# Two one-hot groups in a row ahead of every second expert tile, and four second-half scatter transfers between heads

## The reference, cut to what matters

```
idx = jnp.take_along_axis(cand_idx, top_pos, axis=-1)
gate = jax.nn.softmax(top_s, axis=-1)
u = expert_down[idx]
v = expert_up[idx]
act = jax.nn.gelu(jnp.einsum("td,thkd->thk", xb, u).astype(jnp.float32), approximate=False)
return jnp.einsum("thk,thkd->td", (gate * act).astype(v.dtype), v)
```

## Time and profile before

| | us |
|---|---|
| median of 3 runs | 1308.4 (1308.36 to 1309.39) |
| time of the profiled execution | 1307.0 |
| its span, first to last instruction | 1305.2 |
| PE busy | 1286.4 (99%) |
| PE weight loads busy | 1168.2 (90%) |
| DVE busy | 963.2 (74%) |
| ACT busy | 760.5 (58%) |
| POOL busy | 483.8 (37%) |

### The profile page before, as it was taken

The page is one execution under the profiler, slowest core; times in us unless marked ns, Lnnn a source line. Parts: engine busy times, 40 slices in busy tenths (PEclk is TensorE's granted clock), DMA queues, the critical chain, the costliest instruction groups (busy, mean ns, idle before and its releaser), DMA issues. The chain is left out here.

```text
span 1305.2 us, 25973 instructions
## 1 busy us (share of the span) xinstructions
PE 1286.4 (99%) x8501; PEld 1168.2 (90%) x8501; DVE 963.2 (74%) x1898; ACT 760.5 (58%) x1153; POOL 483.8 (37%) x276
## 2 busy tenths in 40 slices
PE   9999999999999999999999999999999999999997
PEld 8999899999999999998888888888889888888886
DVE  6886677999898468875666666666667668777775
ACT  6833556777777766664555555555474456555556
POOL 1010001888887888887887673000000000000000
PEclk9999999999999999999999999999999999999999
DMA  7459554767776776668888888777664335555551
GB/s 260 148 181 385 210 178 146 191 179 182 174 192 181 191 178 161 161 161 210 215 217 219 217 217 250 242 240 241 225 230 150 114 128 172 187 190 186 186 194 65
DMA packets 119324, 253.00 MB, mean 194 GB/s; under 512 B 44336, under 2 KB 60848, under 8 KB 118752
## 3 DMA queue, kind: packets, MB, share of 16 engines
q1 hardware_dynamic: 77232, 229.24, 53.9%
q0 software_dynamic: 42032, 22.99, 11.2%
HBM read 234.23 MB, written 17.96 MB: 193 GB/s over the span
## 5 line engine op out<-in xcount | busy, mean ns | idle before, releaser
L469 DVE TENSOR_TENSOR wlo<-raw,whi 128x1024 fp32r<-128x1024 f32 (+1 forms) x500 | 508.6, 1033 | 122.4 <-ACT whi L454 111.3
L454 ACT ACTIVATE whi<-raw 128x1024 fp32r<-128x1024 f32 x412 | 434.7, 1057 | 228.2 <-PE ps L476 217.6
L420 POOL DMA_INDIRECT gates_dense<-gate,spot x256 | 472.3, 1845 | 165.0 <-issue 78.4
L474 PE MATMUL ps<-parts,whi 128*128 128x256 f32 x1472 | 422.6, 287 | 2.1 <-DVE parts L561 1.9
L475 PE MATMUL ps<-parts,whi 128*128 128x256 f32 x1472 | 416.2, 283 | 0.0
L476 PE MATMUL ps<-parts,wlo 128*128 128x256 f32 x1472 | 416.2, 283 | 0.0
L474 PEld LDWEIGHTS ps<-parts,whi 128*128 128x128 f32 x1472 | 282.0, 192 | 5.5 <-issue 5.0
L475 PEld LDWEIGHTS ps<-parts,whi 128*128 128x128 f32 x1472 | 282.1, 192 | 0.0
L476 PEld LDWEIGHTS ps<-parts,wlo 128*128 128x128 f32 x1472 | 281.9, 192 | 0.0
L474 PE MATMUL ps<-whi,phi 128*128 128x512 f32 x600 | 234.0, 390 | 3.3 <-DVE plo L1895 2.6
L476 PE MATMUL ps<-whi,plo 128*128 128x512 f32 x600 | 233.6, 389 | 0.0
(11 more groups left out here) (373 smaller groups left out, 1336.0 us busy)
## 6 DMA issues: line engine op xcount, KB each, us to landing
raw<-in_wts SPq DMA_DIRECT2D x412, 512.0 KB
gates_dense<-pf POOLq DMA_DIRECT2D x4, 4096.0 KB, 30.7
gd<-gates_dense SPq DMA_DIRECT2D x22, 256.0 KB, 5.0
gd<-gates_dense SPq DMA_DIRECT2D x10, 512.0 KB, 6.1
gates_dense<-gate,spot POOLq DMA_INDIRECT x256
cst<-in_c POOLq DMA_DIRECT2D x1, 1216.0 KB, 6.4
xt<-in_x_tok SPq DMA_DIRECT2D x2, 512.0 KB, 4.5
kk<-in_keys POOLq DMA_DIRECT2D x1, 1024.0 KB, 5.2
```

The costliest lines, as they stand in the source:

```text
L420: pl.indirect_dma_start(out=dense, out_offset=bass.IndirectOffsetOnAxis(ap=spot[:, tb, h, k:k + 1], axis=0), in_=gate[:, tb, h, k:k + 1], ...
L454: nc.scalar.activation(whi[:, j, :], raw_tile(j // 2, j % 2), ACT.Copy).then_inc(s["w_hi"], 1)
L469: m = nc.vector.tensor_tensor(wlo[:, j, c], raw_tile(j // 2, j % 2)[:, c], whi[:, j, c].bitcast(F32), ALU.subtract)
L474: nc.tensor.matmul(out_ap, wh, xh, start=first, stop=False, skip_group_check=True)
```

## The change

On PE, the steps are taken in pairs: groups n and n+1 stand in a row ahead of tile n for even n, and nothing stands between tiles n and n+1. On ACT, `token_major` in step n copies group n+2 and not n+1. It starts one step earlier, so that groups 0 and 1 are both copied before the first pair. On DVE, the odd steps lay out group n+2 first and do `split_lo` behind it. The even steps keep their order. On POOL, `BETWEEN` is 4 and not 5.

```
-BETWEEN = 5
+BETWEEN = 4
...
                 for n in range(4):
-                    pe.wait_ge(s["ohm"], i * 4 + (n + 1))
-                    if not first or n >= 2:
-                        pe.wait_ge(s["g_mul"], i * 4 + (n - 1))
-                    gate_group(n % 2)
+                    for g in (n, n + 1) if n % 2 == 0 else ():
+                        pe.wait_ge(s["ohm"], i * 4 + (g + 1))
+                        if not first or g >= 2:
+                            pe.wait_ge(s["g_mul"], i * 4 + (g - 1))
+                        gate_group(g % 2)
                     pe.wait_ge(s["w_lo"], i * 4 + (W_EXP + GROUPS_AT + n + 1))
                     pe.wait_ge(s["gelu"], i * 4 + (GROUPS_AT + n - 1))
                     hidden(n, n % 2)
...
                     split_hi(act, None, u % 4, quad + u // 4)
                     if group:
-                        token_major(quad * 4 + (n + 1 - GROUPS_AT), (n + 1) % 2)
+                        token_major(quad * 4 + (n + 2 - GROUPS_AT), n % 2)
...
-                gelu(n, group=n == GROUPS_AT - 1)
+                gelu(n, group=n >= GROUPS_AT - 2)
...
-            last_group = GROUPS_AT + N_GROUPS - 1
+            last_group = GROUPS_AT + N_GROUPS - 2
...
                 for n in range(4):
+                    laid = not last or n < 2
+                    if laid and n % 2:
+                        lay_out(n + 2, i)
                     split_lo(dve, None, (base + n) % 4, i + (base + n) // 4)
-                    if not last or n < 2:
+                    if laid and n % 2 == 0:
                         lay_out(n + 2, i)
                     apply_gates(n, i)
```

More of the change, by code:

```diff
@@ L1300, in gelu @@
                     if group:
-                        token_major(n + 1 - GROUPS_AT, (n + 1) % 2)
+                        token_major(n + 2 - GROUPS_AT, n % 2)
                     act.wait_ge(s["w_used"], W_EXP + n + 1)
```

## The result

The changed kernel takes 1315.07 us in the median of 4 runs (1314.88 to 1315.7), the kernel before 1308.89 in its 4 (1308.36 to 1309.75). The ratio is 1.0048, with a 95% interval of 1.0032 to 1.0063: slower by 6.2 us, where 7.7 was forecast (1316.1 us, range 1312 to 1321). The profiled execution's span is 1313.1 us against 1305.2: 7.9 more. Of the kernel before, the profiled execution (1307.0 us) is faster than any of those 4 runs. Of the 16 runs of the kernel before beside the first experiments, one took 2471.7 us at a lower granted clock; the ratios leave it out.

What follows compares the result with a forecast made beforehand. PE, busy 99% of the span, was taken as the bound. The profiled 1307.0 us, + 9.8 for the late pairs, - 2.1 at the up stage, made 1314.7; with 1.4 to the median, 1316.1 us, range 1312 to 1321.

Steps and rivals of the forecast that it cites:

- Part 1, fewer turns: On PE in the stage with groups: 16 turns from fp16 to fp32 matmuls instead of 32, 1.3 us less.
- Part 2, the chain: ACT waits 2.7 us for the layout, delaying DVE's gates; PE's second group starts at P + 8.2, 1.4 us late.
- How the lateness adds up: On PE, lateness counts once per two pairs: 14.35 us against 13.12, +9.8 us in all, the turns' saving included.
- The short ones: PE stops ahead of groups in the pairs between the long stops: perhaps 7 short ones.
- Part 3, the up stage: At the up stage's start, SP no longer waits for the scatters, so PE's wait goes: -2.1 us.
- The margin: At the up stage's start, PE ready by 594.6, before it needs `plo` at 595.05: 0.45 us.
- the rival with the late up stage: Shifted raw loads or ACT keep the 2.1 us at the up stage: 1318.2 us; chance 0.12.
- The sum: Whole kernel: 1307.0 + 9.8 - 2.1 = 1314.7 us for the profiled execution, 1316.1 for the median, 0.6% slower.
- the 1.4 us added for the median: Whole kernel: the profiled execution was 1.4 us below the median of the runs, so 1314.7 became 1316.1.
- Faster: ACT's stop is absorbed and PE's second group is not late: 1305.0 us; chance 0.08.
- Each pair late by 1.4: The chain runs from PE's second group, so every pair stops: 21 us of stops, 1326.0 us; chance 0.04.
- that rival: PE's stops in the stage with groups make the clock fall to 1.2 GHz: about 50 us, 1366; chance 0.01.

Runs made afterwards that it cites:

- the first experiments: First set of four variants, run beside the kernel before: `BETWEEN` 4 only, pairs with `BETWEEN` 5, layout first, gates before the split; kernel before 1310.11 us.
- gates before the split: The changed kernel with DVE in the order layout, `apply_gates`, `split_lo` in every step; 1303.9 us, ratio 0.996.
- `BETWEEN` alone: The kernel before with `BETWEEN` = 4 instead of 5 and nothing else; 1305.14 us, ratio 0.997.
- layout first: The changed kernel with `lay_out` ahead of `split_lo` on DVE in the even steps too; 1308.54 us, ratio 0.9991.
- split first: The changed kernel with DVE's order as before in every step (split, layout, gates); 1352.53 us in its one run.
- the last experiment: The changed kernel with `apply_gates` ahead of `split_lo` on DVE in every step, and `BETWEEN` = 5 instead of 4; 1308.17 us, ratio 0.9987.

## Why the prediction was right, step by step

- **Part 1, fewer turns.** Forecast 1.3 us by 16 x 0.08. Shown: gates before the split gains 1.2 us on `BETWEEN` alone, 1.5 by the spans, and a pair takes 6.47 where 6.48 was worked out.
- **Part 2, the chain.** Each link came within 0.1 us. In the pair shown, Gelu started at P + 5.10 (forecast 5.01), `split_hi` at 5.36 (5.29), `split_lo` at 6.53 (6.46), the gates ended at 8.18 (8.14), and PE went on at 8.33 (8.2). The last link is the one that was mis-sized: the handover from `apply_gates` to the group took 0.15 and not 0.06. PE's restart itself costs nothing: from the stopped group to the next pair are 6.14 us, and 6.15 was worked out. The 9.0 us of idle time in the view are under the 10 to 11 written down, because the view leaves out 0.18 in each stop. Two pairs take 14.48 and not 14.35. The stage grew by 10.2 us, forecast 9.8. That ACT's stop is the reason was tested from three sides: without it (layout first) PE's idle time goes from 9.0 to 2.4 us; with it in every step it grows to 32.7 and the time by 43; with it but without the pairs it costs nothing. So neither half of the cause is one by itself.
- **How the lateness adds up.** Long and short stops in turn, as forecast, 8 and 7 of them. The short ones I named as possible and left out of the sum. They don't lengthen it, because the chain counts from the start P of a pair: the next pair starts at P + 6.81 and not 6.47, and its second group at P + 8.33 either way. So pairs start 6.81 and 7.67 apart in turn, where 6.5 and 7.9 were forecast.
- **Part 3, the up stage.** Forecast -2.1. Shown: -2.0 by the distance of the first group to the first `phi` matmul with `BETWEEN` alone (478.40 to 594.96, 116.56 against 118.56). In the changed kernel the matmul comes 0.17 after the last expert matmul. Two links in it were wrong. I took the landing of `gd`, 3.5 us, from the kernel before, where SP had waited 3.6 us for the scatters and the weight load ahead of it had long been issued. Freed of that wait, the load is issued 0.1 us behind a 512 KB weight load, and takes 4.8 to 5.1 us in six traces and 5.8 with the split first. It takes 3.7 in the last experiment, where SP waits again. So of the 3.6 us of earlier issue only 2.1 arrive. And with that landing `plo` waits for DVE's own queue (2.68 us from `apply` to `plo`, and as much before: 593.98 to 596.66) and not for ACT's `phi`, as I had it. The margin was nothing and not 0.45, and the gain of 2.1 was just reached: that the rival with the late up stage did not come true was in part luck. That `BETWEEN` has no worth beside the late pairs is shown by the changed kernel with 5.
- **The sum.** +10.2 - 2.1 = 8.1 for the stretch, 7.9 for the span, 7.7 forecast. The medians differ by 6.2, with an interval of 4.2 to 8.2, so the forecast of 7.7 lies in it but on the upper side. The term that was mis-sized is the 1.4 us added for the median. They belong to the kernel before, whose runs spread with their clock, and not to the changed one, whose profiled execution (1314.93) lies within 0.2 of its median. Without them the sum is 1314.7, 0.4 below the measured 1315.07, which is what the stage was short by. Seen by the medians, the change loses the 10.2 us of the stage and gains some 4, as with `BETWEEN` alone and not the 2.1 of the traces, though the interval takes in 2.1 as well. The upper bound was also added up wrongly: 1316.1 + 1.5 + 1.6 + 2.1 is 1321.3 and not 1320.9.
- **The rivals.** "Faster" named its own condition, a second group before P + 6.81; the kernel with the gates ahead of the split meets it and takes 1303.9 us, where the rival gave 1305.0. "Each pair late by 1.4" is excluded by the short stops. The clock did not fall in the changed kernel (1.00 in the stage). But my ground for giving that rival 0.01 was thin. Its price was too high: with the matmuls 0.21 apart, as the split first shows, and not 0.24, half of the stage's 768 would cost 384 x 0.09 = 35 us. The Trainium skill's rule ("TensorE: Matmul & The Clock Gate", A second HAM failure mode), that short idle times between groups of matmuls can make the clock swing, does hold in this very stage once the stops are longer: with idle times of 1.7 to 2.7 us in each pair (split first) the granted clock was 0.50 in places. In the changed kernel, with stops of 1.1 us at most, it stayed up.

## What to carry to other kernels

When an in-order engine is given work on a younger operand (here ACT's copy of a group laid out in the same step), look at what is queued behind it and follow that round trip, with start-to-start times from one step of the trace. It matters only against the time at which the bottleneck engine wants the result, so move producer and consumer together: here another order of three calls on the feeding engine turned 10 us of loss into 1.3 of gain. And when a stage gets faster or slower, ask again which transfer is the last to arrive at its end. A knob that gains 2 us in one version (by the traces; 5 by the medians) gains none in the next and over 4 in the third. And look where the profiled execution lies among its kernel's runs before its distance to the median is carried over to another kernel.

## What the runs showed of the hardware

- A stop of PE ahead of a group costs 0.18 us more than its idle time in the view (0.17 shown, 0.35 lost; 1.03 shown, 1.21 lost). The view counts from the modelled end of the group ahead, 0.50 after its start, and a group that doesn't wait starts after 0.33.
- With stops of about 1.0 us and 0.2 us in turn every 14.5 us the clock stayed at 1.00. With a stop of 1.7 to 2.7 us every 9.7 us ((619.98 - 484.87) / 14) it averaged 0.90 over the stage and fell to 0.50 in stretches between.
- One stop of 2.70 us brought the clock down for some 3 us and cost 1.6 us beside itself; one of 1.92 us at the same place did not, in the one execution traced. In the untraced runs of that kernel the mean clock goes from 0.998 (1307.29 us) down to 0.995 (1311.52 us).
- The 2 x 256 KB of `gd` land after 3.5 and 3.7 us where SP has idled ahead of their issue, and after 4.8 to 5.8 us where they are issued right behind a 512 KB weight load. That the weight load is the reason is argued from these nine traces and wasn't tried by itself.
